# Where the modulation vectors of a two-block transformer are computed, and in what order its expert weights are queued

## The chip, the cores and the metric

One core of a Trainium2 chip runs the whole kernel as one launch. The time is the device time of that core in microseconds (us), the median of several runs. TensorE (PE) multiplies, VectorE (DVE) and ScalarE (ACT) compute element by element, GpSimd (POOL) issues indirect DMAs here, and SyncE (SP) issues nearly all loads of weights, in one order that is fixed when the program is built.

## What is computed

A first block (512 tokens and 16 meta tokens of width 1024): a pooling mixer, a mixture of experts, latent attention, a second mixture of experts. A second block (two layers) whose four sub-layers are modulated by vectors that come from one conditioning vector `c` alone:

```
first_block:   h = h + pool_mixer(...);  h = h + hierarchical_moe(...)     # layer 0
               h = h + mla_mixer(...);   h = h + hierarchical_moe(...)     # layer 1
hierarchical_moe: top-1 of 4 groups, top-2 of its 8 experts;
               (silu(x @ w_gate[e]) * (x @ w_up[e])) @ w_down[e]           # 32 experts, 1024 -> 256 -> 1024
ada_mod(c, w, b):  m = silu(c) @ w + b       # w is 1024 x 3072, four of them
               shift, scale, gate = split(m, 3);  return shift, scale, 1 + gate
second_block:  u = x * (1 + scale) + shift;  y = mixer(u);  x = layer_norm(ALPHA * x + gate * y)
```

The four `ada_w` matrices (12.6 MB each) don't depend on the tokens, so their products can be computed anywhere before they are needed; the first of them is needed where the second block begins.

## The kernel before

All products are fp32. Sixteen stages follow one another: pool, route 0, experts 0, latent, attend, attout, route 1, experts 1, enter, and the second block.

**Loads.** `load_list` writes the order in which SP issues loads, `place_chunks` gives each load a buffer of 1 MB. A load waits on SP until the former content of its buffer has been used, and everything behind it waits too. Outside the expert stages four buffers (`raw0` to `raw3`) take all loads. An expert stage adds twelve: six in the places of the split weights (`raw_in_high`, `raw_in_low`), four in those of the split activations (`raw_in_x`), two behind the routing's scratch (`raw_extra`). Sixteen loads can so be held or under way.

**Experts.** An expert's weights are three chunks of 1 MB. Two experts share a step ("pair"), each with up to 64 token rows, in 64 columns of the PE array each, so their matmuls run side by side. A stage has 24 pairs: 16 of real experts, and 8 for experts that got over 64 rows; a load for one of those is skipped on the chip where no expert needs it, while PE works through the pair all the same. Pairs 3, 6, 9, ... in the order of the program are such ones. In pair j PE does: first half of gate/up of j, transposes of the hidden rows of j-1, transposes of the gathered tokens of j+1, second half of gate/up of j, down projection of j-1. VectorE per pair: `hidden`, a copy of half of the transposed tokens (`x_out`), a copy of half of the result (`rows_out`).

**Modulation.** A modulation matrix comes in 12 pieces of 1 MB (512 output columns by half of the 1024 inputs). Two pieces make one group of 512 outputs. There are two ways to use one:

- on PE, `ada_rows`: 8 matmuls of 128x512 a group, with one column of silu(c) spread over 128 columns as the stationary side, so that all 128 rows of the result are equal; then `ada_pick` on VectorE takes the diagonal of each 128x128 block.
- on VectorE, `ada_piece`: four multiply-adds of 128x512 a piece; then `ada_sums` on PE sums over the partitions, 4 matmuls of one column a group.

Matrices 0 and 1 go through PE: group 0 in the pool stage, three groups in route 0, three in latent, two in route 1, three in enter. Matrix 2 goes through VectorE in attout and route 1, with its sums in route 1 between the ranks and the table. Matrix 3 is done in the second block and isn't touched by the change.

**Routing.** A route stage normalises the rows, transposes them, computes logits on PE, picks experts by a long chain of small VectorE operations, counts ranks on PE (`ranked`), makes positions on VectorE (`places`), the table on PE (`table made`), and then GpSimd gathers rows by that table. The next stage starts, on each engine, when all engines have ended the routing.

Of the kernel before, what the change touches and what calls it, by code (L numbers as in the profile page):

```python
# [164 lines left out]
ADA_COLS = 2 * 3 * D // ADA_PARTS  # L165


def load_list(k):
# [12 lines left out]
    return out  # L181
# [11 lines left out]
def place_chunks(k):  # L193
# [7 lines left out]
    for n, c in enumerate(k.LOADS):  # L201
# [10 lines left out]
        if c in k.MOE0:  # L212
            for w in range(SPLIT_SLOTS):
                for i in range(2):
                    r = RAW_SLOTS + 2 * w + i
                    raw_age[r], raw_holds[r] = n - 2 + (w_age[w] + SPLIT_SLOTS) / (n + SPLIT_SLOTS + 1), w_holds[w]
            for r in range(RAW_IN_W, MOE_RAWS):
                raw_age[r], raw_holds[r] = n - 1 + (r - RAW_IN_W + 1) / 8, after_route(L, r)
        r = min((s for s in raw_age if L is not None or s < RAW_SLOTS), key=lambda s: raw_age[s])
# [263 lines left out]
def pool_vector(k, dve):  # L483
    V = k.V
    bands_vector(k, dve)
# [98 lines left out]
def route_tensor(k, pe, L, T):  # L584
    name = f"route{L}"
    norm_turn(k, pe, name, 0)
# [9 lines left out]
    ada_rows(k, pe, L, 1, 7)  # L596
# [7 lines left out]
    if L == 0:  # L604
        ada_rows(k, pe, 0, 2, 2)
# [11 lines left out]
    if L:  # L617
        pe.wait_ge(*k.after("ada picked", 1, 1))
        ada_rows(k, pe, 1, 2, 7)
# [26 lines left out]
def route_vector(k, dve, L, T):  # L646
# [15 lines left out]
    if L:  # L662
        ada_piece(k, dve, 2, ADA_PARTS - 2)
        ada_piece(k, dve, 2, ADA_PARTS - 1)
# [51 lines left out]
    else:  # L716
        ada_pick(k, dve, 1, 1, 7)
# [53 lines left out]
    if L:  # L771
        ada_done(k, dve, 2)
# [16 lines left out]
    if L:  # L789
        ada_pick(k, dve, 1, 2, 7)  # L790
# [10 lines left out]
    if L == 0:  # L801
        ada_pick(k, dve, 0, 1, 7)
        ada_pick(k, dve, 0, 2, 2)
        ada_pick(k, dve, 0, 3, 3)

# [42 lines left out]
def moe_tensor(k, pe, L, c0):  # L848
# [51 lines left out]
    for j in range(PAIRS + 1):  # L900
        if j < PAIRS:
# [51 lines left out]
def moe_vector(k, dve, L, c0):  # L953
# [86 lines left out]
LATENT_ADA = ((0, 4), (0, 5), (1, 0))  # L1040
# [66 lines left out]
def latent_tensor(k, pe, *_):  # L1107
# [11 lines left out]
    for t in range(XT + 1):  # L1119
        if t % 2 == 0:  # L1120
            if t == 4:
                pe.wait_ge(*k.after("ada picked", *LATENT_ADA[0]))
            ada_rows(k, pe, *LATENT_ADA[t // 2], 6 + t // 2 % 2)
        norm_turn(k, pe, "latent", t)
    for t in range(XT + 1):
# [3 lines left out]
        if t in (2, 3):  # L1129
            pe.wait_ge(*k.after("ada picked", *LATENT_ADA[4 - t]))  # L1130
# [165 lines left out]
def latent_vector(k, dve, *_):  # L1296
    c = k.FIRST[("latent",)]
    def combined(t):
        combine_vector(k, dve, t)
        if t in (2, 4):  # L1300
            ada_pick(k, dve, *LATENT_ADA[t // 2 - 1], 5 + t // 2)
# [3 lines left out]
    ada_pick(k, dve, *LATENT_ADA[2], 6)  # L1305
    ada_done(k, dve, 0)
# [330 lines left out]
def attout_vector(k, dve):  # L1637
    c = k.FIRST[("attout",)]
    split_low(k, dve, c + 1)
    for n in range(6):  # L1640
        ada_piece(k, dve, 2, n)
        if n in (1, 2):
            split_low(k, dve, c + n + 1)
    for half in range(2):
        if half:
            for n in range(6, ADA_PARTS - 2):
                ada_piece(k, dve, 2, n)
# [33 lines left out]
def ada_rows(k, pe, s, g, bank, pieces=None):  # L1681

    for n in pieces or (2 * g, 2 * g + 1):
# [10 lines left out]
def ada_pick(k, dve, s, g, bank):  # L1694
# [3 lines left out]
    for i in range(4):  # L1698
        at = k.PS[:, bank, i * P:(i + 1) * P]
# [1963 lines left out]
```

## Time and profile before

| | us |
|---|---|
| median of 3 runs (2535.94 to 4279.98) | 2537.24 |
| the profiled execution | 2534.56 |
| its span, first to last instruction | 2532.5 |
| PE busy | 2309.3 (91%) |
| VectorE busy | 1246.9 (49%) |
| ScalarE busy | 781.9 (31%) |
| granted PE clock, mean | 0.951 of 2.4 GHz |

The page gives busy times by engine, then the span in 40 slices of 63 us, then the DMA queues, then the chain of work that ended last. The two expert stages are the slices with 363 to 401 GB/s.

### The profile page before, as it was taken

The page shows a single profiled execution, that of the slowest core. Times are in us where ns is not written, and L with a number is a line of the kernel's source. Part 1 is how long each engine was busy: PE and PEld are TensorE (multiplying, and loading weights), DVE is VectorE, ACT ScalarE, POOL GpSimd, SP SyncE. Part 2 cuts the span into 40 slices and gives each one's busy share as a digit, 9 for nine tenths or more (in the row PEclk, how much of TensorE's full clock was granted, in tenths as well). Part 3 has the DMA queues.
Part 4 walks back from the last instruction along what each step waited for, and adds up shares of the span by engine and source line. Part 5 has one row for each costly group of instructions (what it writes and reads, how often), then busy time and mean ns, then how long its engine had stood idle before and what let it go on. Part 6 is the DMA issues. An engine that isn't in the chain of part 4 may idle for free.

```text
span 2532.5 us, 27589 instructions
## 1 busy us (share of the span) xinstructions
PE 2309.3 (91%) x10608; PEld 1586.9 (63%) x10608; DVE 1246.9 (49%) x1906; ACT 781.9 (31%) x1367; POOL 125.7 (5%) x154
## 2 busy tenths in 40 slices
PE   6899997998889999799788999998987888999997
PEld 4533333876744333377567888876666776788886
DVE  5411114556731111578456555558747845633455
ACT  4211113455211111453124232233316642422321
POOL 1111110000001111100000000000000000000000
PEclk9999998999889999899779999999989999999999
DMA  5799996220679998532013443322100031322320
GB/s 204 264 394 401 388 363 234 92 67 1 227 304 399 385 390 335 197 116 94 23 50 108 150 150 127 123 100 84 67 17 1 1 133 67 104 87 100 117 75 34
DMA packets 90850, 416.19 MB, mean 164 GB/s; under 512 B 16600, under 2 KB 16960, under 8 KB 51408
## 3 DMA queue, kind: packets, MB, share of 16 engines
q1 hardware_dynamic: 71024, 373.26, 38.7%
q0 software_dynamic: 19696, 41.17, 4.5%
q8 instruction: 85, 1.39, 0.2%
q14 instruction: 45, 0.37, 0.0%
HBM read 516.34 MB, written 31.98 MB: 217 GB/s over the span
## 4 chain that ended last, share of the span: by engine, by line
PE 74%; DVE 16%; DMA 4%; ACT 3%; issue 2%; SPq 0%; POOL 0%; DVEq 0%; ACTq 0%; POOLq 0%
PE psum L109 15%; PE psum L110 15%; PE psum L111 14%; PE psum L868 13%; PE psum L891 6%; PE psum L1688 2%; DVE w_low L309 2%; PE psum L858 2%; DMA raw_in_x<-in_moe 1%; DMA raw<-in_ada 1%; DVE w_low L1032 1%; DVE ada_sums L1723 1%; ACT w_high L285 1%; DVE gla_head L2361 1%; DMA rows<-in_rows 1%
## 5 line engine op out<-in xcount | busy, mean ns | idle before, releaser
L309 DVE TENSOR_TENSOR w_low<-raw,w_high 128x2048 fp32r<-128x2048 f32 (+2 forms) x110 | 245.5, 2238 | 249.6 <-ACT w_high L285 235.5
L109 PE MATMUL psum<-x_high,w_high 128*128 128x512 f32 x848 | 348.1, 410 | 16.7 <-DVE x_low L1032 9.8
L110 PE MATMUL psum<-x_high,w_low 128*128 128x512 f32 x848 | 339.3, 400 | 0.0
L111 PE MATMUL psum<-x_low,w_high 128*128 128x512 f32 x848 | 337.3, 398 | 0.0
L285 ACT ACTIVATE w_high<-raw 128x2048 fp32r<-128x2048 f32 (+2 forms) x110 | 204.7, 1870 | 297.7 <-PE psum L111 280.5
L111 PE MATMUL psum<-w_low,mlp_high 128*128 128x512 f32 x512 | 202.2, 395 | 0.0
L110 PE MATMUL psum<-w_high,mlp_low 128*128 128x512 f32 x512 | 201.5, 393 | 0.0
L109 PE MATMUL psum<-w_high,mlp_high 128*128 128x512 f32 x512 | 200.5, 392 | 0.9 <-DVE mlp_low L1032 0.9
L109 PEld LDWEIGHTS psum<-x_high,w_high 128*128 128x128 f32 x848 | 160.5, 189 | 64.1 <-ACT u_tile L1818 6.9
L110 PEld LDWEIGHTS psum<-x_high,w_low 128*128 128x128 f32 x848 | 160.2, 189 | 43.8 <-issue 6.3
L111 PEld LDWEIGHTS psum<-x_low,w_high 128*128 128x128 f32 x848 | 160.4, 189 | 39.1 <-issue 0.6
L973 DVE COPY yb<-psum 128x512 f32<-128x512 f32 x48 | 33.2, 692 | 229.7 <-PE psum L891 229.7
L868 PE MATMUL psum<-raw_in_low,xg_turned 128*64 128x512 f32 x288 | 135.4, 613 | 8.4 <-DMA raw_in_low<-in_moe 8.4
L868 PE MATMUL psum<-raw_in_high,xg_turned 128*64 128x512 f32 x288 | 134.1, 609 | 2.1 <-DMA raw_in_high<-in_moe 2.1
L868 PE MATMUL psum<-raw,xg_turned 128*64 128x512 f32 x384 | 130.6, 596 | 1.5 <-ACT xg_turned L922 1.5
L109 PE MATMUL psum<-w_high,x_high 128*128 128x512 f32 (+5 forms) x272 | 103.7, 381 | 29.3 <-DVE x_low L1032 14.1
L940 ACT ACTIVATE yb<-psum 128x512 f32<-128x512 f32 x48 | 28.7, 597 | 309.7 <-PE psum L891 309.7
L960 DVE COPY xg_turned<-psum 128x512 f32<-128x512 f32 x48 | 33.2, 692 | 176.9 <-PE psum L858 176.9
L109 PEld LDWEIGHTS psum<-w_high,mlp_high 128*128 128x128 f32 x512 | 96.3, 188 | 22.7 <-issue 1.1
L110 PEld LDWEIGHTS psum<-w_high,mlp_low 128*128 128x128 f32 x512 | 96.3, 188 | 22.3
L111 PEld LDWEIGHTS psum<-w_low,mlp_high 128*128 128x128 f32 x512 | 96.4, 188 | 20.2
L110 PE MATMUL psum<-w_high,x_low 128*128 128x512 f32 (+5 forms) x272 | 102.4, 376 | 0.0
(552 smaller groups left out, 4120.0 us busy)
## 6 DMA issues: line engine op xcount, KB each, us to landing
raw<-in_moe SPq DMA_DIRECT2D x72, 1024.0 KB
raw_in_x<-in_moe SPq DMA_DIRECT2D x72, 1024.0 KB
raw<-in_mlp SPq DMA_DIRECT2D x64, 1024.0 KB
raw_in_high<-in_moe SPq DMA_DIRECT2D x54, 1024.0 KB
raw_in_low<-in_moe SPq DMA_DIRECT2D x54, 1024.0 KB
raw<-in_ada SPq DMA_DIRECT2D x48, 1024.0 KB
raw_extra<-in_moe SPq DMA_DIRECT2D x36, 1024.0 KB
raw<-in_evin SPq DMA_DIRECT2D x10, 1024.0 KB
```

Of the source, the lines that this page charges most:

```text
L109: pe.matmul(out, ah, bh, start=first, stop=False)
L110: pe.matmul(out, al, bh, start=False, stop=False)
L111: return pe.matmul(out, ah, bl, start=False, stop=last)
L285: act.activation(wh[:, 0:w], raw[:, 0:w], ACT.Copy).then_inc(*k.A.step("high", c))
L309: dve.tensor_tensor(wl[:, 0:w], k.RAW[k.RAW_AT[c]][:, 0:w], wh[:, 0:w].bitcast(F32), ALU.subtract).then_inc(*k.V.step("low", c))
L858: mm = pe.transpose(flat(k, f * P, f * P + P), k.XG[:, j % XG_SLOTS, f * P:(f + 1) * P], const(k, "ident"))
L868: mm = pe.matmul(k.PS[sides[e], 2 + 4 * (j % 2), :], k.XGT[j % 2][:, 4 * part + f, sides[e]], k.RAW[k.RAW_AT[c]][:, f * HALF:(f + 1) * HAL ...
L891: mm = pe.matmul(k.PS[sides[e], 4 + half, :], k.HT[:, f, sides[e]], k.RAW[k.RAW_AT[c]][:, f * D + half * HALF:f * D + half * HALF + HALF], ...
L940: act.activation(k.YB[:, j % 2, HALF:D], k.PS[:, 5, :], ACT.Copy).then_inc(*A.step("moe y", L, j, 1))
L960: dve.tensor_copy(k.XGT[j % 2][:, 4:DK, :].rearrange("p a b -> p (a b)"), k.PS[:, 1, :]).then_inc(*V.step("moe x", L, j, 1))
L973: dve.tensor_copy(k.YB[:, j % 2, 0:HALF], k.PS[:, 4, :]).then_inc(*V.step("moe y", L, j, 0))
L1688: mm = pe.matmul(k.PS[:, bank, :], k.CS[:, f:f + 1].to_broadcast([P, P]), w[:, i * ADA_COLS:(i + 1) * ADA_COLS], start=(f == 0), stop=(f = ...
```

## The change

- `ada_rows` multiplies for 64 output columns at a time: for each of the four 128-column parts of a piece it takes the first and the second 64 columns apart, 256 moving columns each, into partitions 0 to 63 and 64 to 127. A group so gives 128x256 of results in half a PSUM bank. `ada_pick` becomes one multiplication by a folded identity (`SIDE`) and one reduction.
- Six pieces (groups 4 and 5 of matrix 0, group 0 of matrix 1) leave PE in latent for VectorE in experts 0, pairs 9 to 14; the twelve pieces of matrix 2 leave VectorE in attout and route 1 for VectorE in experts 1, pairs 9 to 20. Each group's sums then stand on PE at the head of a pair. Their loads stand in the queue right behind the six chunks of the pair in which they are used.
- Groups 1 and 2 of matrix 1 (four pieces) stand on PE at the head of route 1.
- In the load order the first expert chunks follow the fourth modulation piece; the other four pieces of the start stand among the expert chunks. The buffers that wait for the end of the routing are the last ones to be given.
- PE no longer waits for the other engines' end of the routing at the start of an expert stage.

```diff
+ADA_SIDE = 64
+MOE_PIECES = ([(0, n) for n in range(8, ADA_PARTS)] + [(1, 0), (1, 1)], [(2, n) for n in range(ADA_PARTS)])
+MOE_PIECE_AT = 9
 def load_list(k):
     late = [(s, n) for s in range(2) for n in range(ADA_PARTS)]
-    follow = {0: late[0:8]}
-    follow[k.FIRST[("latent",)] + 1] = late[8:14]
-    follow[k.FIRST[("attout",)] + 3] = [(2, n) for n in range(ADA_PARTS)] + late[14:18]
+    follow = {0: late[0:4], k.MOE0[0] + 3: late[4:6], k.MOE0[0] + 9: late[6:8]}
+    follow[k.FIRST[("attout",)] + 3] = late[14:18]
     follow[k.MOE0[1] + MOE_CHUNKS - 1] = late[18:24]
+    for L, pieces in enumerate(MOE_PIECES):
+        for n, piece in enumerate(pieces):
+            follow.setdefault(k.MOE0[L] + 6 * (MOE_PIECE_AT + n) + 5, []).append(piece)
...
 def place_chunks(k):
...
-                raw_age[r], raw_holds[r] = n - 1 + (r - RAW_IN_W + 1) / 8, after_route(L, r)
+                raw_holds[r] = after_route(L, r)
+                raw_age[r] = (n + MOE_RAWS if raw_holds[r][0][0] == "route done" else -1) + (r - RAW_IN_W + 1) / 8
...
 def route_tensor(k, pe, L, T):
+    if L:
+        for g in (1, 2):
+            pe.wait_ge(*k.after("att done", g - 1))
+            ada_rows(k, pe, 1, g, 3 + g, ADA_HALF)
...
-    if L:
-        for n in range(ADA_PARTS):
-            ada_sums(k, pe, 2, n, 6)
-        pe.wait_ge(*k.after("modulation", 2))
...
 def moe_tensor(k, pe, L, c0):
     for j in range(PAIRS + 1):
+        if 0 <= j - 1 - MOE_PIECE_AT < len(MOE_PIECES[L]):
+            ada_sums(k, pe, *MOE_PIECES[L][j - 1 - MOE_PIECE_AT], 7)
...
 def moe_vector(k, dve, L, c0):
     for j in range(PAIRS + 1):
         if j:
             hidden(j - 1)
+        if 0 <= j - MOE_PIECE_AT < len(MOE_PIECES[L]):
+            s, n = MOE_PIECES[L][j - MOE_PIECE_AT]
+            if n % 2 == 0 and j > MOE_PIECE_AT:
+                ada_taken(k, dve, *MOE_PIECES[L][j - 1 - MOE_PIECE_AT])
+            ada_piece(k, dve, s, n)
         if j + 1 < PAIRS:
             x_out(j + 1)
...
 def ada_rows(k, pe, s, g, bank, at=0):
...
-            mm = pe.matmul(k.PS[:, bank, :], k.CS[:, f:f + 1].to_broadcast([P, P]), w[:, i * ADA_COLS:(i + 1) * ADA_COLS],
-                           start=(f == 0), stop=(f == DK - 1))
+            moving = w[:, i * ADA_COLS:(i + 1) * ADA_COLS].rearrange("p (a q c) -> p q a c", q=ADA_SIDES, c=ADA_SIDE)
+            for q in range(ADA_SIDES):
+                side = slice(q * ADA_SIDE, (q + 1) * ADA_SIDE)
+                mm = pe.matmul(k.PS[side, bank, at:at + 4 * ADA_SIDE].rearrange("p (a c) -> p a c", a=4),
+                               k.CS[:, f:f + 1].to_broadcast([P, ADA_SIDE]), moving[:, q, :, :], start=(f == 0), stop=(f == DK - 1))
...
-UNBARRED = [("tensor", "even_in"), ("tensor", "mlp"), ("tensor", "fox_in")]
+UNBARRED = [("tensor", "moe"), ("tensor", "even_in"), ("tensor", "mlp"), ("tensor", "fox_in")]
```

SP's queue at the start of the program, before (`in_a_w` is the pool stage's weight, `in_ada` a modulation piece, `in_moe` an expert chunk):

```order
L264 DMA raw0_49<-in_a_w 128x2048
L250 DMA raw1_50<-in_ada 128x4x512
L250 DMA raw2_51<-in_ada 128x4x512
L250 DMA raw3_52<-in_ada 128x4x512
L250 DMA raw0_49<-in_ada 128x4x512
L250 DMA raw1_50<-in_ada 128x4x512
L250 DMA raw2_51<-in_ada 128x4x512
L250 DMA raw3_52<-in_ada 128x4x512
L250 DMA raw0_49<-in_ada 128x4x512
L264 DMA raw1_50<-in_moe 128x2048
```

and now:

```order
L259 DMA raw0_49<-in_ada 128x4x512
L273 DMA raw_in_high1_82<-in_moe 128x2048
L273 DMA raw_in_low1_83<-in_moe 128x2048
L273 DMA raw_in_high2_84<-in_moe 128x2048
L273 DMA raw_in_low2_85<-in_moe 128x2048
L259 DMA raw1_50<-in_ada 128x4x512
L259 DMA raw2_51<-in_ada 128x4x512
L273 DMA raw_in_high0_80<-in_moe 128x2048
L273 DMA raw_in_low0_81<-in_moe 128x2048
L273 DMA raw_in_x0_86<-in_moe 128x2048
```

The first expert chunk stood behind eight pieces and in `raw1`, which the fifth piece must leave first; now it stands behind four, in a buffer that nothing has used.

PE between the end of attout and the first pair of experts 1, before (L409 transposes, L580 logits, L599 and L601 ranks, L612 the table, L858 transposes of gathered rows):

```order
L409 MATMUL psum<-const,xn_tiles 128x128 x8
L580 MATMUL psum<-router_w,xf 128x36 x16
L1688 MATMUL psum<-raw_49,condition 128x512 x4
L1688 MATMUL psum<-raw_50,condition 128x512 x4
L599 MATMUL psum<-route_pick,const 128x160
L601 MATMUL psum<-route_pick,const 128x32
L1736 MATMUL psum<-const,ada_sums 128x1 x24
L612 MATMUL psum<-route_block_hot,route_row_hot 128x52 x8
L1688 MATMUL psum<-raw_51,condition 128x512 x4
L1688 MATMUL psum<-raw_52,condition 128x512 x4
L858 MATMUL psum<-const,xg 128x128 x8
```

and now:

```order
L1684 MATMUL psum<-raw_49,condition 64x256 x8
L1684 MATMUL psum<-raw_50,condition 64x256 x8
L1684 MATMUL psum<-raw_51,condition 64x256 x8
L1684 MATMUL psum<-raw_52,condition 64x256 x8
L418 MATMUL psum<-const,xn_tiles 128x128 x16
L590 MATMUL psum<-router_w,xf 128x36 x16
L614 MATMUL psum<-route_pick,const 128x160
L616 MATMUL psum<-route_pick,const 128x32
L623 MATMUL psum<-route_block_hot,route_row_hot 128x52 x8
L860 MATMUL psum<-const,xg 128x128 x8
```

The two groups moved ahead of the transposes, and nothing is left between the logits, the ranks, the table and the first pair (some rows that stay as they are, are left out of both).

VectorE in experts 1 around pair 9, now; before, the rows of L964, L977 and L970 alone repeated there:

```order
L970 TENSOR_TENSOR hidden<-silu,psum 128x256
L1715 TENSOR_SCALAR rows<-raw_in_high_84,condition 128x512
L1718 SCALAR_TENSOR_TENSOR rows<-raw_in_high_84,condition,rows 128x512 x3
L964 COPY xg_turned_138<-psum 128x512
L977 COPY yb<-psum 128x512
L970 TENSOR_TENSOR hidden<-silu,psum 128x256
L1718 SCALAR_TENSOR_TENSOR rows<-raw_in_x_87,condition,rows 128x512
```

A piece stands ahead of `x_out` (L964), which waits until the piece has landed.

## Rows read from the trace of the kernel before

**Rows 1.** The page, part 2, the span in 40 slices of 63 us

```profile
DMA  5799996220679998532013443322100031322320
GB/s 204 264 394 401 388 363 234 92 67 1 227 304 399 385 390 335 197 116 94 23 50 108 150 150 127 123 100 84 67 17 1 1 133 67 104 87 100 117 75 34
```

**Rows 2.** Chain that ended last, experts 0: start us, us, what

```profile
109.32 29.36 DMA raw_in_x<-in_moe
...
249.19 3.58 PE psum L868 x16
252.77 3.43 PE psum L891 x16
256.20 3.43 PE psum L868 x16
260.88 3.58 PE psum L868 x16
```

**Rows 3.** Timeline of PE, both expert stages: start us, us, engine, line [idle before <-releaser]

```profile
106.84 3.65 PE L868 MATMUL psum<-raw,xg_turned 128*64 128x512 f32 x16 [0.77 <-ACT xg_turned L922]
...
147.02 3.51 PE L891 MATMUL psum<-raw_in_x,hidden_turned 128*64 128x512 f32 x14
...
732.27 3.65 PE L868 MATMUL psum<-raw,xg_turned 128*64 128x512 f32 x16 [0.77 <-ACT xg_turned L922]
...
769.29 3.75 PE L891 MATMUL psum<-raw_in_x,hidden_turned 128*64 128x512 f32 x16
```

**Rows 4.** Windows: from:to, length, busy PE, PEld, DVE, ACT, POOL, PEclk, DMA share, GB/s

```profile
120.00:150.00 30.00, 27.20 (x114) 10.66 (x116) 3.19 (x5) 2.83 (x6) 2.02 (x2) 0.89 1.02 420
190.00:225.10 35.10, 35.10 (x177) 13.32 (x176) 5.41 (x9) 5.57 (x13) 6.40 (x7) 1.00 0.97 389
660.00:680.00 20.00, 20.00 (x88) 16.32 (x87) 18.30 (x27) 0.00 (x0) 0.00 (x0) 1.00 0.99 359
```

**Rows 5.** Timeline of VectorE, attout and route 1

```profile
636.62 0.49 DVE L1720 TENSOR_SCALAR ada_sums<-raw,condition 128x512 f32<-128x512 f32 x1 [0.23 <-DVE o_low L1032]
637.15 5.54 DVE L1723 SCALAR_TENSOR_TENSOR ada_sums<-raw,condition,ada_sums 128x512 f32<-128x512 f32 x7
...
714.91 1.22 DVE L769 TENSOR_TENSOR route_row_hot<-route_count,route_place 128x1024 fp32r<-128x1024 f32 x1
```

**Rows 6.** Timeline of PE, pool and both routings

```profile
21.34 10.09 PE L1688 MATMUL psum<-raw,condition 128*128 128x512 f32 x16 [5.27 <-DMA raw<-in_ada]
...
105.01 1.06 PE L858 MATMUL psum<-const,xg 128*128 128x128 f32 x8 [1.24 <-DVE psum L1700]
...
689.35 3.68 PE L409 MATMUL psum<-const,xn_tiles 128*128 128x128 f32 x16 [5.92 <-DVE xn_tiles L386]
...
701.82 7.11 PE L1688 MATMUL psum<-raw,condition 128*128 128x512 f32 x16
...
709.85 7.13 PE L1736 MATMUL psum<-const,ada_sums 128*128 128x1 f32 x48
...
717.39 1.91 PE L612 MATMUL psum<-route_block_hot,route_row_hot 128*128 128x52 f32 x8 [0.41 <-DVE modulation L1752]
...
730.44 1.06 PE L858 MATMUL psum<-const,xg 128*128 128x128 f32 x8 [1.96 <-DVE gate L800]
```

**Rows 7.** Timeline of GpSimd: the first gathers of both routings

```profile
98.27 1.08 POOL L830 DMA_INDIRECT xg<-xn_rows,table  x1 [23.67 <-DVE route_cmp L780]
...
720.69 1.07 POOL L830 DMA_INDIRECT xg<-xn_rows,table  x1 [24.72 <-DVE route_cmp L780]
```

**Rows 8.** Tile `xg`, 95 to 140 us: from issue to landing

```profile
DMA to landing us min/median/max: 4.1/9.6/12.3
```

**Rows 9.** Chain that ended last, latent and enter

```profile
421.15 1.10 DVE psum L1700 x8
...
436.24 6.87 PE psum L1688 x16
...
1062.67 8.09 PE psum L1688 x16
```

More of the change, by code:

```diff
@@ L215, in place_chunks @@
                     r = RAW_SLOTS + 2 * w + i
[L216 removed]
+                    raw_age[r], raw_holds[r] = -2 + (w_age[w] + SPLIT_SLOTS) / (n + SPLIT_SLOTS + 1), w_holds[w]
             for r in range(RAW_IN_W, MOE_RAWS):
[L218 to L219 removed]
+                raw_holds[r] = after_route(L, r)
+                raw_age[r] = (n + MOE_RAWS if raw_holds[r][0][0] == "route done" else -1) + (r - RAW_IN_W + 1) / 8
+        anywhere = L is not None or c in MOE_PIECES[0] + MOE_PIECES[1]
+        r = min((s for s in raw_age if anywhere or s < RAW_SLOTS), key=lambda s: raw_age[s])
         k.RAW_AT[c], k.RAW_AFTER[c] = r, raw_holds.get(r, [])
@@ L802, in route_vector @@
         ada_pick(k, dve, 0, 1, 7)
-        ada_pick(k, dve, 0, 2, 2)
+        ada_pick(k, dve, 0, 2, 7, ADA_HALF)
         ada_pick(k, dve, 0, 3, 3)
+    else:
+        ada_pick(k, dve, 1, 1, 4, ADA_HALF)
+        ada_pick(k, dve, 1, 2, 5, ADA_HALF)
 def store_rows(k, pool, L, T):
@@ L1638, in attout_vector @@
     c = k.FIRST[("attout",)]
[L1639 to L1643, printed above, removed]
+    split_low(k, dve, c + 3)
     for half in range(2):
-        if half:
-            for n in range(6, ADA_PARTS - 2):
-                ada_piece(k, dve, 2, n)
         for t in range(XT):
@@ L1678, in ada_source, with ada_rows @@
     return src[:, 4 * (n % 2):4 * (n % 2) + 4, j * ADA_COLS:(j + 1) * ADA_COLS]
-def ada_rows(k, pe, s, g, bank, pieces=None):
-    for n in pieces or (2 * g, 2 * g + 1):
+def ada_rows(k, pe, s, g, bank, at=0):
+    for n in (2 * g, 2 * g + 1):
         pe.wait_ge(*k.after("raw", (s, n)))
@@ L1687, in ada_rows, with ada_pick @@
             f = 4 * (n % 2) + i
-            mm = pe.matmul(k.PS[:, bank, :], k.CS[:, f:f + 1].to_broadcast([P, P]), w[:, i * ADA_COLS:(i + 1) * ADA_COLS],
-                           start=(f == 0), stop=(f == DK - 1))
+            moving = w[:, i * ADA_COLS:(i + 1) * ADA_COLS].rearrange("p (a q c) -> p q a c", q=ADA_SIDES, c=ADA_SIDE)
[3 more added lines that the diff above has]
+                               k.CS[:, f:f + 1].to_broadcast([P, ADA_SIDE]), moving[:, q, :, :], start=(f == 0), stop=(f == DK - 1))
         mm.then_inc(*k.T.step("raw free", (s, n)))
     k.T.mark("ada rows", s, g)
-def ada_pick(k, dve, s, g, bank):
+def ada_pick(k, dve, s, g, bank, at=0):
     dve.wait_ge(*k.after("ada rows", s, g))
     dve.wait_ge(*k.V.now())
-    for i in range(4):
-        at = k.PS[:, bank, i * P:(i + 1) * P]
-        dve.scalar_tensor_tensor(out=at, in0=at, scalar=1.0, in1=const(k, "ident"),
-                                 op0=ALU.mult, op1=ALU.mult, accum_out=k.MODC[:, s, 4 * g + i:4 * g + i + 1]).then_inc(
-            *k.V.step("ada picked", s, g))
+    rows = k.PS[:, bank, at:at + 4 * ADA_SIDE].rearrange("p (a c) -> p a c", a=4)
+    dve.tensor_tensor(rows, rows, k.SIDE[:, :].unsqueeze(1).to_broadcast([P, 4, ADA_SIDE]), ALU.mult).then_inc(*k.V.step())
+    dve.wait_ge(*k.V.now())
+    dve.tensor_reduce(k.MODC[:, s, 4 * g:4 * g + 4], rows, AX.X, ALU.add).then_inc(*k.V.step("ada picked", s, g))
 def ada_total(k, s, n):
-    return k.ACC[:, :] if s == 3 else k.ACC6[:, n // 2, :]
+    return k.ACC[:, :] if s == 3 else k.ROWB[:, 0, 0:ADA_COLS]
 def ada_piece(k, dve, s, n):
@@ L1737, in ada_sums, with ada_taken @@
     mm.then_inc(*k.T.step("ada sums", s, n))
+def ada_taken(k, dve, s, n):
+    g = n // 2
+    dve.wait_ge(*k.after("ada sums", s, n))
+    dve.tensor_copy(k.MODC[:, s, 4 * g:4 * g + 4], k.PS[:, 7, 4 * g:4 * g + 4]).then_inc(*k.V.step())
 def ada_done(k, dve, s):
@@ L3384, in program @@
     k.SQR1 = k.at("route_squares_late", [P, D], k.XLAT)
-    k.ACC6 = k.at("ada_sums", [P, ADA_PARTS // 2, ADA_COLS], k.end)
     k.GATE = k.at("gate", [P, 2, XT + 1], k.keep)
@@ L3390, in program @@
     k.AID = k.at("assignments", [P, 4 * (XT + 1)], k.end, I32)
+    k.SIDE = k.at("side_ident", [P, ADA_SIDE], k.end)
     k.XG = k.at("xg", [P, XG_SLOTS, D], k.SCR)
```

37 lines of the change are left out of this document (10 added, 27 removed).

## The prediction

> **What bounds the kernel now.** The page comes first. PE is busy for 2309 of 2532 us; in its 40 slices the transfers are near their ceiling in two places alone, at 363 to 401 GB/s, and those are the two expert stages [rows 1]. The pieces that the change moves are loaded in slices 7 and 11, latent's start and attout, at 234 and 227 GB/s. So the change takes transfers and VectorE work out of stretches with room, and puts them where the transfers have the least.
>
> The chain of waits, next, shows what sets the pace there: in experts 0 it runs over PE's matmuls without a gap, and a pair, from the second half of one gate/up to that of the next, takes 260.88 - 249.19 = 11.69 us [rows 2]. The windows give the reserve: three pairs are 35.1 us, PE is busy in all of them, and the transfers have a share of 0.97 and 389 GB/s. That is 13.65 MB per three pairs (twelve chunks of 1.05 MB, the third pair being one whose loads are skipped, and 1.07 MB of rows). Where PE waited for transfers, from 120 to 150 us, they reached 420 GB/s [rows 4]. The stage is bound by PE, with the transfers 7% behind it.
>
> The timeline of PE shows how the stages begin. From the first gate/up to the second down projection a regular pace needs 8.26 + 11.69 + 8.26 = 28.2 us (8.26 is a pair less one 3.43 us projection [rows 2]); it takes 147.02 - 106.84 = 40.2 in experts 0 and 769.29 - 732.27 = 37.0 in experts 1 [rows 3]. So 12.0 and 8.8 us are lost to chunks that are late; the chain has one transfer of 29.36 us there [rows 2].
>
> **The terms**, against the profiled execution's 2534.56 us.
>
> *Pool and route 0: -3.5.* Group 0 is 16 matmuls in 10.09 us at the start [rows 6]. With 64 output columns on each side of the array the same group is 16 side-by-side steps of 256 columns; the expert matmuls, two at a time at 64 columns, show what such a pairing gives: 16 steps of 512 columns for both in 3.43 us [rows 2], where 16 full-width matmuls take 7.11 [rows 6]. So about half, -5 for group 0. At the other end the first turn of rows waits 1.24 us on an `ada_pick` [rows 6]; PE no longer waits for it. But what PE waits for next in pool are the normalised rows, which aren't faster. Bounds 0 and -5, and I lean to the gain.
>
> *Start of experts 0: -9.* Ten expert chunks stand in the queue before the routing ends, against none that could be issued before the fifth piece's buffer was empty. Bounds: all of the 12.0, and 5, if the chunks come late because they share the transfers with four pieces that now stand among them. I take three quarters.
>
> *Sums in experts 0: +3.* 48 sums took 7.13 us [rows 6], 1.19 a group; three groups, 3.6, a little less at full clock. They stand at the head of a pair on PE, beside nothing.
>
> *Pieces in experts 0: +8.* The transfers of three pairs need 13.65 MB / 0.420 = 32.5 us. A piece has shorter runs; the stretch in which little but pieces was loaded ran at 359 GB/s at a share of 0.99 [rows 4], so three pieces are 3.15 / 0.359 = 8.8 us. Together 41.3, against 35.1 + 1.5 x 1.19 = 36.9 of PE: 4.4 us a round of three pairs. Experts 0 has two such rounds, 8.8 us; bounds 0 (the lead hides it) and 14 (7 a round, at the 389 GB/s of before instead of 420). Sixteen buffers give a lead, but it is spent within each round already: two pairs with loads ask for 12.6 MB, 30 us at 420 GB/s, in 23.4 us, and the third gives it back. I take +8.
>
> By the Trainium skill, DMA: Bandwidth & Descriptors, the table at its head, a core's share of HBM is about 358 GB/s and the fabric's ceiling 435 GB/s. By the first, 16.8 MB would take 46.9 us a round, 10 more than PE; by the second 38.6, hardly a loss. The 420 GB/s of this trace [rows 4] speaks for the second as the limit of a core that runs alone, but the pieces' 359 keeps me between them.
>
> *Latent: -5.5.* One group's 6.87 us and a pick's 1.10 are on the chain [rows 9], and a second pick is of the same kind: -9.1 at most. Where these matmuls are gone PE waits for the normalisation instead, partly at the lower clock; -2 is the other bound. In between.
>
> *Attout: 0.* The ten pieces on VectorE lay beside PE, which was busy for all of 660 to 680 us [rows 4].
>
> *Route 1: -6.6.* After the places (714.91 + 1.22 = 716.13) the table began at 717.39, having waited for modulation 2 [rows 5, 6]: -1.3. From the first gather to the turn of its rows passed 730.44 - 720.69 = 9.75 us, with a wait on `gate`, the end of the routing [rows 6, 7]; the shortest gather lands in 4.1 [rows 8], and PE is no longer held: -5.7. A pick in VectorE's chain: -1.1. Against it, the two groups now stand ahead of the transposes. PE was idle there for 5.92 us [rows 6], and two half groups take about 7.1: +1.5, since more than that idle is asked. The matmuls that leave from between logits and ranks lay beside VectorE's choice of experts, and bring nothing. Bounds -10 and 0: if the gather takes the median 9.6 [rows 8], the 5.7 is gone.
>
> *Start of experts 1: -6.5* of 8.8, as above, bounds -8.8 and -3.
>
> *Sums in experts 1: +6* (six groups at 1.0). *Pieces in experts 1: +20*: four rounds at 4.4 are 17.6, and 2.4 for PE's clock, which was 0.89 in the stretch with gaps [rows 4]; bounds 0 and 28.
>
> *Enter: -2.* One group on the chain takes 8.09 [rows 9], half of it -4; the loads of those six pieces now stand behind more, +2.
>
> VectorE's own part, 0.49 + 3 x 0.79 = 2.86 or 4 x 0.79 = 3.17 us a piece [rows 5], costs nothing: it is busy for 5.41 of 35.1 us [rows 4], and with 9 more still has 20 free. If that cover goes, it is the last rival.
>
> Sum: -3.5 - 9 + 3 + 8 - 5.5 - 6.6 - 6.5 + 6 + 20 - 2 = +3.9, so 2538.5 in a profiled execution. The median of before is 2.7 above its profiled execution: **2541 us**.
>
> **The rivals.** 2% (51 us) is about what a measurement of this kernel can tell from no change.
>
> *The lead hides the pieces' loads* (0.26). The skipped pairs fall between, and the stages end with pairs that have no pieces, in which buffers fill again. For it: PE waited nowhere in the stretches of 35.1 us, so at 0.97 the buffers still were ahead. Against: the arithmetic of 41.3 to 36.9. Then the +28 falls away: 2541 - 28 = 2513.
>
> *Heavier rounds* (0.14). Transfers at 389 GB/s beside pieces at 359: 35.1 + 8.8 = 43.9, 7.0 over PE, six rounds 42 instead of 28, and the clock at 0.89 in more of them, about 8: 2541 + 14 + 8 = 2563. If instead the earlier chunks bring nothing at the stages' starts, the 15.5 is gone, 2556, which lies here too.
>
> *VectorE holds the next pair's rows* (0.07), the one that ends slower. The piece of pair j stands ahead of `x_out(j+1)`, but its load stands behind the down chunks of pair j, which PE needs a pair later. When the transfers fall behind, the piece lands last, `x_out(j+1)` waits, PE's next gate/up waits for it, and no buffer comes free: the lead can't be used at all. Each of the 12 pairs with loads and a piece then runs at its transfers: 6.3 MB / 0.420 + 1.05 / 0.359 = 17.9 us, and 0.5 of rows' share is in that; against 11.69 and about 0.8 of sums, 5.4 more each, 65. In the six skipped ones PE waits for piece and copy, about 2 each: 77 in place of 28, 2541 + 49 = 2590. It decides from the point where a piece lands over 6.5 us after its pair's first half gate/up (11.69, less 1 for `hidden`, 3.2 for the piece and 1 for the copy). For it: the order of the queue. Against: a chunk may be loaded up to 16 buffers ahead, and in the stretch before none was late.
>
> *More than 2% faster* (0.03): all gains at their bounds and no loss, 2541 - 28 - 20 = 2493, is not even that; it would need something that I don't see.
>
> **How the numbers follow.** The forecast has 0.50: all between the ends of its terms, 2526 to 2554. The range takes in the hidden loads with 5 us below them, 2508, and the heavier rounds with 5 above, 2568; the 0.07 of the last rival, the 0.03 and the tails stay out. Faster by over 2% (below 2486) 0.03; slower by over 2% (above 2588) 0.07: about the weight of the last rival; within 2% the rest, 0.90.
>
> **What the profile after would show.** The first down projections within 33 us of the stages' first gate/up confirm the early chunks. In pairs 9 to 14 and 9 to 20: PE's waits on expert chunks and the transfers at a share of 1.0 and 410 GB/s confirm the forecast, a pair spacing of 12.1 us without waits confirms the hidden loads. Waits of PE on `xg_turned` and of VectorE on a piece's load show the last rival. In route 1 the table should start right after the places, and the turn 5 to 6 us after the gather's issue; in latent and enter the half groups should take 3.5 us. I would be wrong above all if the rate beside the pieces is not the 420 and 359 that I join from two stretches, or if the waits among buffers, which no row of before shows, cost more than either.

## The result, and the profile after

| | us |
|---|---|
| the changed kernel, median of 4 runs (2577.94 to 2590.22) | 2585.41 |
| the kernel before, median of 4 runs (2535.94 to 4279.98) | 2541.97 |
| ratio, with its 95% interval | 1.0173 (1.0134 to 1.0211) |
| spans of the two profiled executions | 2575.9 and 2532.5 |

The change makes the kernel 1.7% slower, 43 us; the interval reaches from 1.3% to 2.1%. The forecast was 2541 in a range of 2508 to 2568: as good as no change (+3.9 in the sum), where the two traces differ by 43.4 us. One execution of the kernel before took 4279.98 us, and no trace shows why; the other three lie within 11 us. The argument below rests on the lengths of stages inside a trace: PE's granted clock in the pool stage isn't the same in all traces, which moves everything behind it by some 8 to 11 us (see the last section), and totals carry that.

The page, part 2, of the changed kernel (answers to [rows 1]):

```profile
DMA  7799994210459999632102342332100032222320
GB/s 274 290 378 364 386 365 170 75 66 1 166 224 396 384 385 373 244 125 82 49 33 75 146 177 103 145 115 82 67 17 1 1 115 82 90 98 98 109 80 33
```

The work moved where it was meant to: slices 1 and 2 (the early chunks) transfer more, slices 7 and 11 less. But the expert stages move no more per second than before, 364 to 396 GB/s, though they have more to move. They are longer instead.

The chain of waits through pairs 8 to 11 of experts 0, start us, us, what (answers to [rows 2]):

```profile
221.35 3.43 PE psum L870 x16
226.03 3.58 PE psum L870 x16
229.61 3.46 PE psum L893 x16
233.07 16.80 DMA raw_in_high<-in_ada
255.63 3.58 PE psum L870 x16
```

The regular spacing ends. The down projection ends at 233.07, in that moment a modulation piece is sent for, and 16.80 us pass until it lands. The timeline of VectorE shows who waits for it:

```profile
249.89 0.49 DVE L1715 TENSOR_SCALAR rows<-raw_in_high,condition 128x512 f32<-128x512 f32 x1 [12.92 <-DMA raw_in_high<-in_ada]
250.41 2.33 DVE L1718 SCALAR_TENSOR_TENSOR rows<-raw_in_high,condition,rows 128x512 f32<-128x512 f32 x3
252.66 0.68 DVE L964 COPY xg_turned<-psum 128x512 f32<-128x512 f32 x1
```

VectorE stands for 12.92 us, and `x_out` (L964), which PE needs for its next gate/up, comes 3 us behind the landing. The timeline of SP in the same stretch shows what else stood still:

```profile
233.07 0.38 SPq L259 DMA_DIRECT2D raw_in_high<-in_ada  x1
234.99 1.73 SPq L270 DMA_DIRECT2D raw_extra<-in_moe  x2
...
238.50 0.08 SPq L270 DMA_DIRECT2D raw_in_high<-in_moe  x1
250.86 0.39 SPq L259 DMA_DIRECT2D raw_in_low<-in_ada  x1
```

The rows of L270 are the six loads of pair 12, which are skipped on the chip: they carry no byte, and take six buffers. The next load with bytes needs the buffer that pair 10's down projection frees, at 250.86; SP's waits from 222 to 330 us have this one as the longest of the pieces' line:

```profile
SPq L259 <- PE psum L893: 32.0, 4, 12.3
```

The windows (columns as in [rows 4]) show the transfers run dry meanwhile:

```profile
236.00:244.00 8.00, 8.00 (x33) 3.56 (x34) 0.97 (x3) 0.53 (x2) 2.03 (x2) 0.79 1.02 418
244.00:250.00 6.00, 6.00 (x30) 2.01 (x28) 0.11 (x1) 0.45 (x1) 0.00 (x0) 1.00 0.54 197
257.10:292.20 35.10, 30.17 (x136) 11.82 (x134) 7.87 (x14) 3.71 (x8) 4.48 (x5) 0.90 1.02 413
900.10:935.20 35.10, 29.59 (x128) 10.65 (x126) 8.89 (x16) 3.71 (x8) 4.74 (x5) 0.88 0.91 359
970.30:1005.40 35.10, 29.81 (x147) 12.99 (x144) 13.33 (x22) 4.58 (x10) 5.44 (x5) 1.00 0.95 378
```

In the last three windows PE is busy for 30 of 35 us, where it was busy for all of them before [rows 4]. Three candidates are visible at once: VectorE's wait, a queue that stands still behind empty buffers (the last two windows have shares of 0.91 and 0.95), and plain bytes (the one before them has 1.02). The experiments had to separate them.

Where the 43.4 us between the two traces arise, read from the same instruction in both (`turn` is the first transpose of gathered rows of a pair):

| stretch | forecast | measured |
|---|---|---|
| start to the turn of pair 0, experts 0 | -3.5 | -2.7 |
| to the turn of pair 9 | -9 | -8.7 |
| to the end of experts 0 | +11 | +23.0 |
| latent to PE's last matmul of attout | -5.5 | +0.9 |
| from there through route 1, to the turn of pair 0 | -6.6 | -6.8 |
| to the turn of pair 9, experts 1 | -6.5 | -1.7 |
| to the end of experts 1 | +26 | +34.9 |
| enter and the second block | -2 | +4.5 |

### The profile page after: what moved, and what is told of

It is laid out like the page before. It is cut to its first block, busy times and chain, and to the rows that moved or that the text cites. A ratio compares the mean times of both kernels' runs of the same rounds, so it can differ in the third digit from the quotient of the medians.

```text
span 2575.9 us, 27779 instructions
## 1 busy us (share of the span) xinstructions
PE 2280.5 (89%) x10728; PEld 1589.9 (62%) x10728; DVE 1257.0 (49%) x1861; ACT 782.4 (30%) x1367; POOL 128.4 (5%) x154
## 3 DMA queue, kind: packets, MB, share of 16 engines
q1 hardware_dynamic: 71024, 373.26, 37.7%
## 4 chain that ended last, share of the span: by engine, by line
PE 69%; DVE 17%; DMA 7%; ACT 4%; issue 2%; POOL 0%; DVEq 0%; ACTq 0%; SPq 0%; POOLq 0%
PE psum L109 15%; PE psum L110 15%; PE psum L111 15%; PE psum L870 11%; PE psum L893 5%; DVE w_low L318 2%; DMA raw<-in_moe 1%; PE psum L860 1%; DMA raw<-in_ada 1%; DVE w_low L1043 1%; ACT w_high L294 1%; DVE rg_in L2363 1%; DVE gla_head L2363 1%; DMA raw_extra<-in_ada 1%; DMA raw_in_low<-in_ada 1%
## 5 line engine op out<-in xcount | busy, mean ns | idle before, releaser
L870 PE MATMUL psum<-raw_in_low,xg_turned 128*64 128x512 f32 x296 | 147.5, 644 | 7.4 <-DMA raw_in_low<-in_moe 7.4
L870 PE MATMUL psum<-raw_in_high,xg_turned 128*64 128x512 f32 x296 | 143.7, 631 | 2.7 <-ACT xg_turned L926 1.8
L977 DVE COPY yb<-psum 128x512 f32<-128x512 f32 x48 | 33.1, 689 | 165.0 <-PE psum L893 165.0
L870 PE MATMUL psum<-raw_in_x,xg_turned 128*64 128x512 f32 x408 | 108.8, 606 | 4.2 <-DMA raw_in_x<-in_moe 4.2
L111 PE MATMUL psum<-w_low,x_high 128*128 128x512 f32 (+5 forms) x272 | 101.4, 373 | 0.0
```

What stands on the lines that cost most here:

```text
L111: return pe.matmul(out, ah, bl, start=False, stop=last)
L870: mm = pe.matmul(k.PS[sides[e], 2 + 4 * (j % 2), :], k.XGT[j % 2][:, 4 * part + f, sides[e]], k.RAW[k.RAW_AT[c]][:, f * HALF:(f + 1) * HAL ...
L977: dve.tensor_copy(k.YB[:, j % 2, 0:HALF], k.PS[:, 4, :]).then_inc(*V.step("moe y", L, j, 0))
```

## The experiments

All times of pieces below are the length of a stage from the turn of pair 3 to the end of its last down projection, in the profiled execution. Before, it is 259.2 us in experts 0 and 260.7 in experts 1; in the changed kernel 285.3 and 300.2. Ratios are against the kernel before, executed beside each group of experiments (its medians are 2538.3 to 2543.3).

The expectations weigh four theories. T1: VectorE waits for a piece that is sent for late, and holds up the next pair's rows. T2: the bytes of the pieces. T3: VectorE's work on the pieces. T4: skipped loads hold buffers, and the queue stands still behind them.

**1. Use a piece one pair later.**

```diff
+MOE_USE_AT = MOE_PIECE_AT + 1
-        if 0 <= j - MOE_PIECE_AT < len(MOE_PIECES[L]):
-            s, n = MOE_PIECES[L][j - MOE_PIECE_AT]
+        if 0 <= j - MOE_USE_AT < len(MOE_PIECES[L]):
+            s, n = MOE_PIECES[L][j - MOE_USE_AT]
```

(and the same in `moe_tensor` for the sums; the load list keeps `MOE_PIECE_AT`)

> The changed kernel with one edit: VectorE uses a piece (and PE sums a group) one pair later than its load's place in the queue. Its loads stand where they stood. Theory T1 (the piece can't be sent for before the down projection of two pairs earlier frees its buffer, so it is issued when its own pair begins, lands some 14 to 17 us later, and x_out of the next pair waits behind it on VectorE): with a pair more of time, 11.7 us, the piece is there or nearly there when VectorE comes to it. Most of the about 50 us that pairs 9 to 21 of the two stages lost beyond their sums comes back: 2540 to 2548 against 2585, VectorE's waits on pieces under 3 us each. Theory T2 (bytes: 16.8 MB per three pairs are more than the transfers give in PE's time): the lateness moves from pieces to chunks and about 28 us stay: 2560 to 2570.

Measured: 2573.64, ratio to before 1.0125 (1.0091 to 1.0159). The stages take 280.1 and 300.2. VectorE's waits between 222 and 320 us:

```profile
DVE hidden L971 <- PE psum L1732: 1.9, 1, 1.9
DVE rows L1716 <- DMA raw_in_high<-in_ada: 0.4, 1, 0.4
```

The 12.9 us waits are gone (0.4 is left), and yet PE got back 5.2 us, not 45. It now waits for chunks:

```profile
PE psum L871 <- DMA raw_in_low<-in_moe: 3.5, 1, 3.5
PE psum L871 <- DMA raw_in_x<-in_moe: 3.0, 2, 1.7
```

T1 fails as the main cause: the most visible wait of the trace was mostly a symptom. T2's number, 2560 to 2570, isn't reached either.

**2. Keep a piece's wait, drop its work.**

```diff
+    if s != 3:
+        dve.wait_ge(*k.V.now())
+        dve.tensor_scalar(acc[:, 0:8], w[:, 0:8], k.CS[:, 0:1], None, ALU.mult).then_inc(*k.V.step())
-    for i in range(4):
+    for i in range(4 if s == 3 else 0):
```

> The changed kernel with the work of a piece in the expert stages taken out, its load and its wait kept: VectorE multiplies 8 columns of one quarter in place of four times 512 (the modulation vectors of matrix 2 and half of the others are so not computed). T1: in a pair that waits, the chain is load issued, landing, piece, x_out, gate/up, down, next load issued; it is shorter by 3 us wherever it sets the pace, about nine pairs: 2585 - 27 = 2558, range 2552 to 2566. T2 (bytes): VectorE's work isn't in the chain, 2580 to 2586. A third theory, T3, that it is VectorE's work and not the wait that delays x_out, would give all back, 2535.

Measured: 2581.84, ratio 1.0158 (1.0125 to 1.0191); the stages take 285.2 and 296.5, 3.8 us less than with the work. That is T2's number. The kernel leaves out VectorE's work, 18 times some 3 us, and gains next to nothing: this refutes T3, and T1 once more as the main cause.

**3. Keep the work, drop the loads.**

```diff
-    for L, pieces in enumerate(MOE_PIECES):
-        for n, piece in enumerate(pieces):
-            follow.setdefault(k.MOE0[L] + 6 * (MOE_PIECE_AT + n) + 5, []).append(piece)
...
+        blank = const(k, "ones").unsqueeze(1).to_broadcast([P, 4, P])
```

> The changed kernel without the 18 loads of pieces in the expert stages; VectorE does the same multiply-adds on a constant, PE the same sums (the modulation vectors concerned are so wrong). T1 and T2 both: no wait is left but the sums, 2585 - 50 = 2535 (2530 to 2540). T3, VectorE's work delays x_out: it stays near 2585 - 10.

Measured: 2533.25, ratio 0.9964 (0.9945 to 0.9983); 267.2 and 270.0. As all theories but T3 said. This is the floor for what follows: with the pieces' work and sums and the early chunks, without a byte of them. Over it the changed kernel has 18.1 + 30.2 = **48.3 us** (the forecast had 28), the kernel of experiment 1 has 43.1.

**4. The early chunks alone**, on the kernel before.

```diff
-    follow = {0: late[0:8]}
+    follow = {0: late[0:4], k.MOE0[0] + 3: late[4:6], k.MOE0[0] + 9: late[6:8]}
...
-                raw_age[r], raw_holds[r] = n - 1 + (r - RAW_IN_W + 1) / 8, after_route(L, r)
+                raw_holds[r] = after_route(L, r)
+                raw_age[r] = (n + MOE_RAWS if raw_holds[r][0][0] == "route done" else -1) + (r - RAW_IN_W + 1) / 8
```

(and the same base of -2 for the six buffers of the split weights)

> The kernel before with the new order of the first loads alone: expert chunks behind the fourth piece, buffers that wait for the routing last. Its matmuls, pieces and barriers are those of before. From the changed kernel's trace, in which the chunks' start gained 12.5 us in experts 0 and gave 3.3 back at pair 5, and gained 6.5 and gave 3.7 back in experts 1: 2542 - 9 - 3 = 2530 (2525 to 2535). If the early chunks are only fast because the pieces of latent and attout no longer compete, 2540.

Measured: **2528.20, ratio 0.9941 (0.9918 to 0.9965)**: 0.6% faster than the kernel before, small but clear of the scatter. The chain that ended last in it, at the start of experts 0:

```profile
107.27 3.65 PE psum L869 x16
111.95 7.02 PE psum L869 x32
120.20 3.58 PE psum L869 x16
123.79 3.43 PE psum L892 x16
131.90 3.58 PE psum L869 x16
135.48 3.43 PE psum L892 x16
142.79 22.61 DMA raw<-in_moe
```

From the first gate/up to the second down projection now pass 135.48 - 107.27 = 28.2 us, the regular 28.2, against 40.2 [rows 3]. But a chunk then takes 22.61 us and pair 5 is 3.3 us late. This hiccup is in the changed kernel too, in both stages (14.9 and 16.2 us in place of 11.7).

**5. No skipped loads** (96 loads left out that the chip skips with this input).

```diff
-        out.append(c)
+        if k.CH[c][0] is not None:
+            out.append(c)
...
-                               k.RAW[k.RAW_AT[c]][:, f * HALF:(f + 1) * HALF], start=(part == 0 and f == 0), stop=(part == 1 and f == 3))
+                               k.RAW[k.RAW_AT[c]][:, f * HALF:(f + 1) * HALF] if here else blank(), ...
```

> The changed kernel without the 96 loads that are skipped on the chip (for the experts over 64 rows, of which this input has none); PE does the same matmuls for those pairs on a constant. No byte less is transferred, but the skipped loads no longer take six of sixteen buffers each time. Theory T4 (in each round of three pairs the queue stands still behind buffers that skipped loads hold empty, and the transfers run dry for some 4 us): the rounds with pieces go from about 45 to 41 us, six of them, and the hiccup at pair 5 (3.3 and 4.5 us) goes too: 2585 - 24 - 7 = 2554. Theory T2 (bytes alone, 16.8 MB a round): 2578 to 2585. T1 (the piece's wait on VectorE): 2575.

Measured: 2552.79, ratio 1.0048 (1.0025 to 1.0072), as T4 said. The stages take 273.3 and 282.8. The hiccup at pair 5 is gone (11.69 us in both), which is worth 3.3 + 4.4; with it taken out of the floor too, 26.6 us are left of 48.3. Not one byte less was transferred: the pages of both kernels have 373.26 MB on the queue of these loads. The edit takes SP's time for issuing the skipped loads away together with their buffers; that the buffers are what counts is read from SP's wait above, 12.3 us for a down projection of PE, where the six issues were done within 4 us.

**6. Both: no skipped loads, a piece used one pair later.** The edits of 1 and 5.

> Two edits of the changed kernel together: a piece is used one pair later (alone 2574), and the skipped loads are left out (alone 2553). What then is left beyond the sums can only be bytes: 16.8 MB a round at 413 GB/s are 40.7 us against PE's 36.8, six rounds, 23, less what the lead of the buffers hides. If bytes bind, 2550 to 2556, no better than without the skipped loads alone. If it is the wait of VectorE for a piece sent for late (T1) that is left in that kernel, where pairs of 20.25, 16.9, 17.0 and 18.6 us remain, they go: 2530 to 2540.

Measured: 2542.06, ratio 1.0011 (0.9988 to 1.0034), between the two forecasts. The stages take 268.3 and 280.5, 19.3 us over the floor. Windows over the pairs with pieces:

```profile
257.10:292.20 35.10, 32.89 (x162) 15.83 (x160) 11.94 (x19) 4.68 (x10) 5.68 (x5) 1.00 1.02 414
900.10:935.20 35.10, 33.11 (x163) 12.71 (x160) 13.45 (x21) 4.96 (x11) 6.67 (x6) 1.00 1.02 415
935.20:970.30 35.10, 34.09 (x169) 15.22 (x167) 12.64 (x22) 5.17 (x11) 5.79 (x5) 1.00 1.02 410
```

The transfers' share is 1.02 in all six windows from 222 to 327.3 and from 865 to 970.3 us, at 407 to 419 GB/s, where the changed kernel had 0.88 to 0.95 in four of the same. The transfers never pause here, and VectorE waits for no piece between 222 and 330 us. What is left is bytes.

**7. Pieces spread over the stages**, each used in its own pair.

```diff
+MOE_PIECE_PAIR = ([3 * n + 5 for n in range(6)], [2, 4, 6, 8, 10, 11, 12, 14, 16, 18, 20, 22])
-            follow.setdefault(k.MOE0[L] + 6 * (MOE_PIECE_AT + n) + 5, []).append(piece)
+            follow.setdefault(k.MOE0[L] + 6 * MOE_PIECE_PAIR[L][n] + 5, []).append(piece)
```

> The changed kernel with its 18 pieces spread over the stages: in experts 0 with pairs 5, 8, 11, 14, 17, 20, in experts 1 with pairs 2, 4, 6, 8, 10, 11, 12, 14, 16, 18, 20, 22, each used in the pair behind whose chunks it is loaded, as now. The bytes of three pairs are 14.7 MB in experts 0 and 15.2 in experts 1 in place of 16.8, so 35.6 and 36.9 us at the 413 GB/s of the rounds with pieces, against PE's 35.1 and a half to one sum. T2: nearly nothing is lost but the sums, 2585 - 50 + 8 = 2543 (2537 to 2552). T1 (every piece is sent for when its pair begins and lands 14 us later, x_out behind it): each of the 18 still costs its wait, 2570 to 2585.

Measured: 2590.52, ratio 1.0198 (1.0147 to 1.0249); 289.0 and 300.8, or 52.6 over the floor, with bytes that by the expectation's sum nearly fit. T2 fails here and T1 holds, with more than it asked for. VectorE's timeline at pair 8 of experts 1:

```profile
870.05 3.11 DVE L1719 SCALAR_TENSOR_TENSOR rows<-raw_in_low,condition,rows 128x512 f32<-128x512 f32 x4 [14.41 <-DMA raw_in_low<-in_ada]
873.08 0.68 DVE L964 COPY xg_turned<-psum 128x512 f32<-128x512 f32 x1
```

**8. Spread, and used one pair later.** The edits of 7, with the use as in 1.

> The kernel with the pieces spread over the stages (2590), each used one pair later. Bytes can't be what cost it 48 us, since a round had 14.7 to 15.2 MB; its pairs with a piece took 20 us where VectorE had waited for it, 11 to 15 us each. T1: the waits go, 2590 - 40 = 2550, or less. T4 (the queue stands behind skipped loads): some of the holes stay, 2560 to 2570. If neither, 2585 or more.

Measured: 2558.20, ratio 1.0082 (1.0052 to 1.0112); 272.1 and 290.0, 24.9 over the floor: just short of what T4 forecast, and over T1's 2550. The wait on VectorE was worth 27.7 us in this arrangement and 5.2 in the changed kernel: where bytes and queue leave slack, it binds alone; where they don't, it hides behind them.

**9. Half the bytes a piece**, on the kernel of experiment 1.

```diff
+        parts = DK // 2 if c[0] == 3 or c in late_rows() else DK // 4
+        sync.dma_start(k.RAW[r][:, 0:parts * ADA_COLS].rearrange("p (f w) -> p f w", f=parts), ada_source(k, *c)[:, 0:parts, :]).then_inc(
```

> The kernel that uses a piece one pair later (2574), its 18 loads cut to half a megabyte each (two of four quarters; VectorE multiplies these twice, so the modulation vectors concerned are wrong). As many loads, buffers and operations, 1.57 MB less a round. T2 (bytes): 4 us less in each of six rounds, 2574 - 24 = 2550. T4 (the queue stands still where six buffers are held by skipped loads, whatever a piece weighs): the block lasts as long, 2566 to 2572.

Measured: 2561.30, ratio 1.0102 (1.0056 to 1.0147): over T2's number, under T4's. The profiled execution is one of those with the lower clock in the pool stage (0.53 from 30 to 58 us, against 0.97 from 30 to 47 in experiment 1), which disturbs the total. The stages take 279.4 and 283.0, 25.2 over the floor in place of 43.1. So 9.4 MB less gave 17.9 us. Bytes count even while the queue stands still behind skipped loads; neither theory alone is right.

**10 to 12. What the rest of the change is worth without the pieces**: the kernel of experiment 4 with the 64-wide `ada_rows` and the folded `ada_pick`; the same with `("tensor", "moe")` in `UNBARRED`; the same with one group moved in enter:

```diff
-    ada_rows(k, pe, 1, 4, 2)
     spread_tensor(k, pe, 0, 0)
+    ada_rows(k, pe, 1, 4, 2)
```

> The kernel before with the early expert chunks (2528 in its own run) and with the 64-wide modulation matmuls and the folded diagonal; pieces and barriers as before. From the traces: pool 1.7 less, one group on the chain in latent and one in enter, each 3.4 to 4 less, route 1 about 1: 2528 - 9 = 2519 (2515 to 2524). If PE only waits for VectorE instead, 2526.

> The kernel above, and PE no longer waits at the start of an expert stage for the other engines' end of the routing. In the changed kernel's trace the first turn of rows came 5.9 us earlier against the gather's issue in experts 1 and about 1 in experts 0, of which 2 to 3 us were lost again to the lower clock of the first gate/up: 3 to 5 less than the kernel above, 2515. If the next gather or the lower clock takes it all, equal.

> The kernel with early chunks, 64-wide modulation matmuls and no barrier for PE (2533), with one group of the last six pieces multiplied behind the first turn of rows in place of ahead of it, so that the next two weight loads are sent for after the scatter and the gathers of the rows. In the trace without this edit the last scatter took 5.4 us and the gathers 11.3 beside transfers at 418 GB/s, where the scatter took 2.1 in the kernel before. If that collision is what eats the shorter matmuls' gain in enter: 2533 - 5 = 2528. If not, equal.

Measured: 2532.99, 2533.13 and 2535.09, ratios 0.9973 (0.9951 to 0.9995), 0.9989 (0.9961 to 1.0016), 0.9992 (0.9969 to 1.0015), against 0.9941 for the early chunks alone. All three expectations of a gain miss: none of the three edits is measurably better than the kernel of experiment 4. The traces show gains that are lost again. In the second, PE reached enter 5.0 us ahead of experiment 4, and the second block only 2.8 ahead; its chain there:

```profile
1018.49 5.44 DMA expert_rows<-yb,table
1025.19 11.28 DMA expert_row_pairs<-expert_rows
```

where experiment 4 has

```profile
1023.52 2.07 DMA expert_rows<-yb,table
```

In the trace of experiment 4 no load runs beside the scatter (0 to 1 GB/s from 1023 to 1026 us); in the second of these kernels loads do, from 1019 us on, at 408 GB/s from 1021. Experiment 12 was to part them and didn't: in its trace the loads run at 117, 354 and 410 GB/s from 1024 to 1027 us, beside a scatter that takes 5.71. So the collision is neither confirmed nor refuted by it.

The rest of the loss isn't in the traces. The profiled execution of experiment 11 took 2525.25, less than the 2528.91 of experiment 4; its ten executions reach from 2525.25 to 2544.28, the seven of experiment 4 from 2522.90 to 2531.41. The pool stage's clock (last section) would do this, but no trace was taken of the slower executions.

## Why the prediction was wrong

**The step that failed** is the one on the pieces in the expert stages: "+8" and "+20", from 41.3 us of transfers against 36.9 of PE in a round of three pairs. It was 48.3 us in place of 28. That is half of the miss: 20.3 us more would have given 2561, inside the range. The rest of the 39.5 us between the sum's +3.9 and the traces' 43.4 is latent (6.4), enter (6.5) and the start of experts 1 (4.8), each outside its bounds or against its sign, and small remainders. The experiments take the 48.3 us apart:

- *Bytes: 19.3 us* (experiment 6 over the floor). The prediction's arithmetic for this part, 4.4 us a round of which the lead hides some, is of the right size: 3.2 a round. That the transfers go at 407 to 419 GB/s there, between the 420 and the 359 that it joined, is right too.
- *Skipped loads that hold buffers: 22 to 24 us* (48.3 - 26.6, or 43.1 - 19.3). The prediction said that sixteen buffers give a lead. With seven loads a pair they are 2.3 pairs deep, and behind a skipped pair six of them are empty. In each round the queue then stands before a buffer of a pair that PE has not finished, itself late for want of data. The prediction named "the waits among buffers, which no row of before shows" as what would prove it wrong, but gave them no price. The trace of before did have a hint: 389 GB/s over three pairs where 420 was possible [rows 4] was read as even slack, but behind the loads of a skipped pair the transfers went at 414 GB/s from 225 to 255 us and then paused, while PE was busy:

```profile
255.00:258.00 3.00, 3.00 (x16) 1.01 (x14) 0.72 (x2) 0.87 (x2) 0.21 (x1) 1.00 0.54 150
```

- *VectorE's wait: 5 to 7 us* (48.3 - 43.1, or 26.6 - 19.3). This is the last rival, "VectorE holds the next pair's rows", which had a chance of 0.07 and a price of 2590. Its mechanism is there: a piece is sent for when its pair begins. Its argument against, that a chunk may be loaded 16 buffers ahead, is the one that failed. But its price was wrong as well: that 2590 is near the measured 2585 is chance. Had only the trace been read, it would have been believed.

**The other steps.**

- *Start of experts 0, -9*: right, -8.7. All of the 12 us came (28.2 us in experiment 4), and 3.3 went at pair 5 to skipped loads, as experiment 5 shows. The prediction discounted for another reason.
- *Start of experts 1, -6.5*: -1.7, outside the bounds. The hiccup cost 4.5, and PE's clock 2.7: the timeline of PE after the gather,

```profile
729.01 1.91 PE L623 MATMUL psum<-route_block_hot,route_row_hot 128*128 128x52 f32 x8 [6.17 <-DVE route_row_hot L772]
736.09 1.97 PE L860 MATMUL psum<-const,xg 128*128 128x128 f32 x8 [5.18 <-DMA xg<-xn_rows,table]
738.83 1.12 PE L870 MATMUL psum<-raw_in_high,xg_turned 128*64 128x512 f32 x1 [0.77 <-ACT xg_turned L926]
```

  The turn takes 1.97 us in place of 1.06 [rows 6] and a matmul 1.12 in place of 0.64. PE stood idle for 6.17 and 5.18 us just before, where a group of modulation matmuls used to lie; the granted clock from 730 to 736 us is 0.50, the lower level. The prediction gave the removal of these matmuls no price. In experiment 10 the group still stands before the turn, but shorter, with 6.58 us in place of 9.36: PE then idles for 3.66 us in place of 1.96 [rows 6], the turn takes 1.94 us, and 7.87 us pass to the next turn where it was 5.42 (8.08 in the changed kernel). So the shorter group alone goes with most of this loss.
- *Route 1, -6.6*: right, -6.8. The two groups at its head take 7.13 us and cost 1.1 of them (the prediction had 1.5): the first transposes start 7.0 us behind the last matmul of attout, where it was 5.92 [rows 6]. That hides a gain that the prediction had at nothing under *Attout*: without pieces VectorE ends the first normalised rows 2.1 us behind that matmul, in place of 5.9. The table starts right behind the places (727.74 + 1.22 = 728.96, then 729.01) and the turn comes 736.09 - 732.30 = 3.8 us after the gather's issue, in place of 9.75 [rows 6, 7]:

```profile
732.30 1.07 POOL L832 DMA_INDIRECT xg<-xn_rows,table  x1 [23.74 <-DVE route_cmp L781]
```

- *Latent, -5.5*: +0.9 up to the end of attout. The group and the picks are off the chain, but other things lengthened it:

```profile
418.08 11.54 DMA yc<-expert_rows
...
452.08 1.97 PE psum L418 x8
454.05 0.27 PE psum L109
```

  The load of `yc` takes 11.54 us where the chain before had 8.33. And PE comes to the first projection cold: 1.97 for the turn where it was 0.87, 0.27 a matmul where it was 0.15. That the lower clock could take part of the gain was said (bound -2); that nothing would be left was outside the bounds. Why that load is slower stays open. Some 3 us more were lost between there and attend, which no experiment explains.
- *Enter, -2*: +4.5. The last pieces were sent for late, and the scatter went beside them:

```profile
1066.10 6.67 DMA expert_rows<-yb,table
...
1074.02 14.11 DMA expert_row_pairs<-expert_rows
```

  The transfers are at 393 to 415 GB/s from 1066 to 1088 us; in the kernel before, the scatter takes 2.06 us with at most 1 GB/s beside it. That this collision is the cause is argued from the traces only: the slow scatters of this kernel and of experiments 10 to 12 all lie beside loads, the fast ones of before and of experiment 4 don't, and no run has the one without the other.
- *The sums*, +3 and +6: 8 matmuls in 1.05 us, and in experiment 3 a pair with sums takes 12.83 us in place of 11.69. So 1.14 each, 3.4 and 6.8: right.

By the Trainium skill, DMA: Bandwidth & Descriptors, the table at its head, a core has some 358 GB/s of HBM and the fabric 435; the 407 to 419 GB/s over whole rounds (experiment 6) are above the first and just under the second, as the 420 of before was. No run here has a second core at work.

## What to carry to other kernels

Count the depth of an in-order load queue in buffers that hold data: a load that may be skipped takes its buffer all the same, and adding one load to every step can cost more through that than through its bytes. When a trace shows several late things at once, take the waits away one by one and both together; the longest one can be a symptom, and a rival whose total comes out right can still have the wrong cause. Work that fills an engine's idle time in front of a critical step can be what keeps its clock up, so shortening it or moving it off isn't free.

## What was not expected of the hardware

PE's clock in the pool stage differs between traces of nearly the same program: 0.97 from 30 to 47 us in experiment 1, 0.53 from 30 to 58 in experiment 9, with the first big matmul of that stage at 47.4 and 58.3 us. It shifts all that follows by 8 to 11 us, as much as most edits here bring.

The record has a pattern here that no experiment was made for. From 30 to 47 us the clock is 1.00 in both traces with the 128-wide group 0 (before and experiment 4). Of the twelve traces with the 64-wide one, eight have 0.95 to 1.00 and four (experiments 5, 7, 8 and 9) 0.50 to 0.56. From 20 to 30 us PE is busy for 8.3 to 8.7 us in the first two and for 5.4 to 6.5 in the twelve. So halving those matmuls may have put the clock at risk in front of the stage; two traces against twelve don't prove it. The pool term of the prediction (-3.5, measured -2.7) came out in an execution with the faster pool stage: in the four others the first turn of rows comes at 110.6 to 112.4 us, 5.6 us or more behind the 105.01 of before.
